# Layer norm after the convolution: eight channel tiles added on VectorE before one product with ones, in place of eight accumulated products

## The reference, cut to what matters

```python
def _layernorm(x, g, b, eps):
    mu = jnp.mean(xf, axis=-1, keepdims=True)
    var = jnp.mean(jnp.square(xf - mu), axis=-1, keepdims=True)
    y = (xf - mu) * lax.rsqrt(var + eps) * g + b

def _conv_branch(val, gate, og, conv_k, conv_b, ln_g, ln_b, w_o):
    u = val * jax.nn.sigmoid(gate)
    u = _causal_depthwise_conv(u, conv_k, conv_b)
    u = _layernorm(u, ln_g, ln_b, LN_EPS)
    u = jax.nn.silu(u) * jax.nn.silu(og)
    return u @ w_o
```

## Time and profile before

| | us |
|---|---|
| median of 3 runs | 1135.39 (1134.3 to 1137.38) |
| the profiled execution's own time | 1135.28 |
| its span in the trace | 1133.5 |
| PE busy, share of the span | 1074.1, 95% |
| DVE busy | 809.3, 71% |
| ACT busy | 637.7, 56% |
| mean granted TensorE clock | 0.994 of 2.4 GHz |

### The profile page before, as it was taken

How to read it: one execution, slowest core, us unless ns; L and a number is a source line. 1 busy time by engine, 2 the same in 40 slices (tenths; PEclk the granted TensorE clock), 3 DMA queues, 4 the chain that set the end, 5 groups by cost and what they waited for, 6 DMA issues and landing times.

```text
span 1133.5 us, 25869 instructions
## 1 busy us (share of the span) xinstructions
PE 1074.1 (95%) x10950; PEld 1006.2 (89%) x10950; DVE 809.3 (71%) x1329; ACT 637.7 (56%) x898; POOL 6.5 (1%) x15
## 2 busy tenths in 40 slices
PE   4999999999999998899999988999999999999997
PEld 3999889898989887899999978889889888889997
DVE  4964577757666775787677675789889889955573
ACT  5844565535444664655455556656658567667343
POOL 0000000000000000000000000000000000000000
PEclk9999999999999999999999989999999999999999
DMA  7552266676844441436555734333323232224531
GB/s 244 155 181 90 70 209 232 223 273 213 285 154 149 157 140 38 146 133 205 185 185 173 234 108 152 113 113 113 113 81 124 99 105 85 76 76 133 196 119 38
DMA packets 132991, 167.69 MB, mean 148 GB/s; under 512 B 2657, under 2 KB 124513, under 8 KB 131489
## 3 DMA queue, kind: packets, MB, share of 16 engines
q1 hardware_dynamic: 131632, 153.51, 41.6%
q0 software_dynamic: 1264, 12.78, 2.8%
HBM read 164.18 MB, written 2.10 MB: 147 GB/s over the span
## 4 chain that ended last, share of the span: by engine, by line
PE 79%; DVE 12%; ACT 6%; issue 2%; DMA 1%; SPq 0%; DVEq 0%; ACTq 0%
PE bank L310 16%; PE bank L311 14%; PE bank L312 14%; DVE wl L272 2%; PE banks L616 2%; PE bank L620 2%; PE bank L618 2%; PE bank L616 2%; PE banks L620 2%; PE banks L618 2%; ACT wh L267 2%; DVE hf L2364 2%; PE bank L652 1%; PE banks L1126 1%; PE bank L1158 1%
## 5 line engine op out<-in xcount | busy, mean ns | idle before, releaser
L310 PE MATMUL bank<-xh,wh 128*128 128x256 f32 x1360 | 397.7, 292 | 0.6 <-DVE wl L272 0.6
L311 PE MATMUL bank<-xl,wh 128*128 128x256 f32 x1392 | 393.5, 283 | 0.0
L312 PE MATMUL bank<-xh,wl 128*128 128x256 f32 x1360 | 384.3, 283 | 0.0
L272 DVE TENSOR_TENSOR wl<-raw,wh 128x2048 fp32r<-128x2048 f32 x97 | 221.4, 2286 | 83.4 <-ACT wh L267 83.3
L310 PEld LDWEIGHTS bank<-xh,wh 128*128 128x128 f32 x1360 | 259.9, 191 | 9.8 <-issue 2.8
L311 PEld LDWEIGHTS bank<-xl,wh 128*128 128x128 f32 x1392 | 266.5, 191 | 0.8 <-issue 0.7
L312 PEld LDWEIGHTS bank<-xh,wl 128*128 128x128 f32 x1360 | 260.2, 191 | 0.0
L267 ACT ACTIVATE wh<-raw 128x2048 fp32r<-128x2048 f32 x97 | 184.6, 1906 | 48.7 <-PE bank L620 38.8
L296 DVE TENSOR_TENSOR wl<-raw,wh 128x1024 fp32r<-128x1024 f32 x86 | 103.7, 1217 | 22.9 <-ACT wh L288 22.7
L2364 DVE SCALAR_TENSOR_TENSOR hf<-big,vecs,hf 128x256 f32<-128x256 f32 x240 | 101.4, 478 | 0.0
L288 ACT ACTIVATE wh<-raw 128x1024 fp32r<-128x1024 f32 x86 | 87.6, 1057 | 8.8 <-PE bank L312 5.5
(11 more groups left out here) (393 smaller groups left out, 2234.4 us busy)
## 6 DMA issues: line engine op xcount, KB each, us to landing
raw<-in_ffn_w_up SPq DMA_DIRECT2D x44, 1024.0 KB, 5.1
raw<-in_w_in SPq DMA_DIRECT2D x36, 1024.0 KB, 5.5
raw<-in_ffn_w_down SPq DMA_DIRECT2D x22, 1024.0 KB, 5.0
raw<-in_gla_w_in SPq DMA_DIRECT2D x12, 1024.0 KB, 6.1
big<-in_ada_w POOLq DMA_DIRECT2D x8, 1536.0 KB, 8.3
raw<-in_attn_w_qkv SPq DMA_DIRECT2D x6, 1024.0 KB, 5.0
raw<-in_gla_w_out SPq DMA_DIRECT2D x4, 1024.0 KB, 5.1
raw<-in_attn_w_out SPq DMA_DIRECT2D x4, 1024.0 KB, 5.1
```

The source lines that it names most:

```text
L272: eng.tensor_tensor(WL[:, n % RING, :, :], RAW[:, n % RING, :, :], WH[:, n % RING, :, :].bitcast(F32), ALU.subtract).then_inc(w_lo_ready, 1)
L310: nc.tensor.matmul(ps, wh, xh, start=start, stop=False)
L311: nc.tensor.matmul(ps, wh, xl, start=False, stop=False)
L312: return nc.tensor.matmul(ps, wl, xh, start=False, stop=stop)
```

## The change

Each group of eight products with ones becomes one DVE instruction, which adds the eight tiles into one tile `LNP` of 128 x 256, and one product of ones with `LNP`. `LNP` is tile 63 of the big buffer. DVE reads the eight tiles through a rearranged view: for each token it goes over the eight tiles, so successive elements lie 256 elements (1024 bytes) apart. DVE's `ln` now has a step 0 (it follows the last taps on the same engine) and a step 2 (it waits for ACT's squares).

```diff
+        LNP = tiles(63, 1)[:, 0, :]
@@
             def ln(step):
                 if step == 0:
-                    pe.wait_ge(sem("conv_done"), 1)
                     pe.wait_ge(sem("gn_rstd"), 5)
-                    for g in range(KT):
-                        last = nc.tensor.matmul(PS[2][:, 0:T], ones, CONV[:, g, :], start=g == 0, stop=g == KT - 1)
-                    last.then_inc(sem("ln_sums"), 1)
-                if step == 3:
-                    pe.wait_ge(sem("ln_squares"), 1)
-                    for g in range(KT):
-                        last = nc.tensor.matmul(PS[2][:, 0:T], ones, S8[:, g, :], start=g == 0, stop=g == KT - 1)
-                    last.then_inc(sem("ln_sums"), 1)
+                if step in (0, 3):
+                    pe.wait_ge(sem("ln_tiles_added"), 2 if step else 1)
+                    nc.tensor.matmul(PS[2][:, 0:T], ones, LNP, start=True, stop=True).then_inc(sem("ln_sums"), 1)
@@
                 if last == TAPS:
                     ch.all()
-                    dve.sem_inc(sem("conv_done"), 1)
 
             def ln(step):
+                if step in (0, 2):
+                    src = CONV
+                    if step == 2:
+                        dve.wait_ge(sem("ln_squares"), 1)
+                        src = S8
+                    v.tensor_reduce(LNP, src.rearrange("p k t -> p t k"), AX_X, ALU.add)\
+                        .then_inc(sem("ln_tiles_added"), 1)
                 if step == 1:
```

## The result

The changed kernel takes 1139.66 us (median of 14 runs, 1137.59 to 1142.91), the kernel before in the same comparison 1136.93 (14 runs, 1134.29 to 1138.6). The ratio is 1.0035, 95% interval 1.0024 to 1.0047: slower by 2.7 to 5.3 us. Forecast was 1133.9, and the time lies above the range's end of 1138.2.

What follows compares the result with a forecast made beforehand. Layer norm on ACT and DVE was taken to set the time from 1005 to 1017 us. Of 3.03 + 3.02 us taken from PE, 2.86 and 1.75 return as idle, leaving 1.44: 1133.9 us, range 1131.8 to 1138.2.

Steps and rivals of the forecast that it cites:

- 7.05 us predicted from L1803 to the root's end: Second place, ACT's queue: nothing waits after L1803, so root L1322 ends at 1008.22 instead of 1009.66.
- the 1.44 us gained: Behind the second place: root, DVE's scaling, ACT's silu and L1158 all come 1.44 us earlier.
- r: Time of one DVE reduction adding eight tiles, 2048 elements per partition, at both places; taken as 2.29 us.
- my own formula: Both reductions lie on the path: the kernel's change is -1.44 + 2 (r - 2.29) us.
- the first rival: At both places the strided read is slow: slower kernel from r = 3.01, 1138.2 us at r = 4.43; chance 0.14.
- its turning point of 3.01: Reduction time r, in us, at which the forecast change of the kernel is zero.
- its doubled case: Both reductions at twice the price per element: r = 4.43 us, kernel 1138.2 us.
- The rival of the clock: TensorE's clock falls in PE's new gaps, of 2.8 and 2.6 us; kernel 1135.4 us, chance 0.18.
- the fall behind the first gap: After PE's 2.8 us idle at the first place: low clock hidden, as PE is 1.75 us ahead of ACT.
- Behind the second gap I had 1.5: After PE's 2.6 us gap before L1167: half clock costs 1.5 us, not hidden, as L1158 is due at once.
- the two rivals: The slow strided read, chance 0.14, and TensorE's clock falling in the new gaps, chance 0.18.
- the gap before the first product: First place: PE sits idle 2.8 us from 990.3 while DVE's reduction runs.

Runs made afterwards that it cites:

- the kernels with the gap filled: Changed kernel plus unused PE products in the first idle gap, or in both gaps; ratios to the kernel before 1.0024 and 1.0022.
- second only: Kernel before with only the second group of products replaced by a strided reduction and one product; ratio to the kernel before 1.0014.
- with the first gap filled: Changed kernel plus eight unused PE products ahead of PE's wait at the first place; ratio to the kernel before 1.0024.
- second trace of the changed kernel: Changed kernel run again unchanged for one more profiled execution; 1142.29 us, stretch from last mask to product behind silu 30.91 us.
- both gaps filled: Changed kernel plus eight unused PE products in the first gap and four before the inverse's product; ratio to the kernel before 1.0022.
- in order: Changed kernel with both reductions reading the same elements as they lie, summing eight neighbouring tokens instead of tiles; ratio to the kernel before 0.9991.
- late: Changed kernel with the second strided reduction moved on DVE behind the state's copy and the inverse's level; ratio to the kernel before 1.0004.
- the shared version: Against the kernel before, PE and DVE split both sums, DVE adding in order and, at the second place, behind the copy; ratio 0.9977.

## Why the prediction was wrong

- **What bounds the stretch** was right. The layer norm on ACT and DVE sets the time from the copy L2483 to the product behind silu: 7.05 us predicted from L1803 to the root's end, 7.03 measured, and 1.19 of the 1.44 us gained in mask to root where the reductions had the assumed length.
- **The step that failed is the size of r.** I took 2.29 us, by rows that read in order, though I had written that only the access pattern isn't that of these rows. Measured: 3.58 and 3.77. In my own formula that is -1.44 + 1.29 + 1.48 = +1.33, slower. It is the first rival, to which I gave 0.14, with r between its turning point of 3.01 and its doubled case. By that step alone the time would have been 1135.39 + 1.33 = 1136.7, slower and yet inside the range.
- **The rival of the clock was right in kind and wrong in place and sum.** I called the fall behind the first gap hidden. It is, for the work of PE between the groups, but not for the product that DVE waits for (1.19 instead of the 0.70 of the kernels with the gap filled) nor for the results that ACT needs before it squares. Filling the gaps took out 0.83 in mask to root, against the trace where only the first gap was followed by the low clock. Behind the second gap I had 1.5; measured were 1.2 (second only, and with the first gap filled) and 2.19 (9.35 against 7.16, second trace of the changed kernel).
- **I took the two rivals one at a time.** They feed each other: a longer reduction makes the gap before the first product 3.97 us instead of 2.8. 1.48 us of the stretch are what the reductions' length leaves (both gaps filled, 28.13 against 26.65), and 0.8 to 2.8 the clock's (28.95 and 30.91 against 28.13). Together 2.3 to 4.3, against 2.7 to 5.3 timed; the second trace's sum lies well inside, the first's just below. How often each case comes is open, with two traces and the hint of the timed runs.
- **The base moved.** The forecast started from 1135.39, the median of 3 runs; in the comparison the kernel before took 1136.93. From that base the forecast would have been 1135.4 and the range would have ended at 1139.7, so that the time lies above the range is in part the base. That it went the wrong way is not: 1.4 us faster was forecast, and it is 2.7 to 5.3 slower.
- **The rules of the Trainium skill.** The Trainium skill's "SBUF — State Buffer", in the note on cachelines, was the one to follow: accesses that go to a new line each pay. The runs agree and give the price for DVE, 1.67 ns instead of 1.04 for an element, with the exception over two tiles. "VectorE: DVE Perf Modes" in the Trainium skill, perf-mode tier table, has the reduction at one element per cycle; that holds in order only (2.29), and the measurement decides against it for the stride. The table at the end of "TensorE: Matmul & The Clock Gate" in the Trainium skill asks for no idle gaps of PE above about 3 us. I read that as shorter ones being harmless, and that did not hold here: 2.5, 2.7 and 1.8 us (second only, in order, late) were each followed by the low level.

## What to carry to other kernels

Price a reduction by the order in which it reads its elements before its count: if no row of the trace has that stride, take the slower end as likely, or rearrange the sum into adds of whole tiles. Products taken off the busiest engine gained nothing here while it then waited for the engine that took them over; let both work at once and leave the last add to the product, as the shared version does. And look at what is queued behind a new instruction: a serial chain's copy behind it is late by its full length (ACT stood still 4.03 us for it), and every new gap of TensorE must be priced with the clock behind it.

## What the runs showed of the hardware beyond that

A strided tensor_tensor of 2048 elements, three strided views, takes 4.45 us against 2.29, a reduction 3.59. With two elements per output the stride of 1024 bytes is free (0.69 both), with four it is not (1.88 against 1.22). The low clock came behind gaps of 1.8 to 4.0 us and stayed for 3 to 7 us; in the changed kernel it did not come behind a second gap of 2.0 us in one execution and did behind one of 2.5 in the other, and it did come behind the 1.84 us of the late kernel. So the length of a gap alone does not tell it.
